# Expert blocks: rows turned a step ahead, overflow blocks with weight buffers of their own and conditional row transfers

## The reference

```python
def expert_block(args):
    xblk, e = args
    h = jax.nn.silu(xblk @ w_gate[e]) * (xblk @ w_up[e])
    return h @ w_down[e]

yb = lax.map(expert_block, (xb, blk_expert))
y = yb.reshape(P, D) * buf_gate[:, None]
return jax.ops.segment_sum(y, buf_tok, num_segments=T + 1)[:T]
```

## Time and profile before

| | |
|---|---|
| median of 3 runs | 3824.81 us (3824.13 to 3830.76) |
| the profiled execution | 3824.16 us |
| its span | 3822.2 us |
| TensorE busy (products) | 3326.4 us, 87% |
| VectorE, ScalarE, GpSimd busy | 39%, 19%, 20% |
| share of the 16 DMA engines, queue of SP | 26.9% |
| share of the 16 DMA engines, queue of POOL | 5.9% |
| expert stage of layer 0 | about 827 to 1250 us |
| expert stage of layer 1 | about 2127 to 2554 us |

### The profile page before, as it was taken

The page is one execution under the profiler, slowest core; times in us unless marked ns, Lnnn a source line. Parts: engine busy times, 40 slices in busy tenths (PEclk is TensorE's granted clock), DMA queues, the critical chain, the costliest instruction groups (busy, mean ns, idle before and its releaser), DMA issues. The chain is left out here.

```text
span 3822.2 us, 37209 instructions
## 1 busy us (share of the span) xinstructions
PE 3326.4 (87%) x14316; PEld 2289.4 (60%) x14316; DVE 1501.4 (39%) x2645; ACT 713.8 (19%) x1630; POOL 778.9 (20%) x483
## 2 busy tenths in 40 slices
PE   6979999959997499999998799936979989789996
PEld 5848666744444376676666344424757757578842
DVE  4374613320102444566654100025477631465502
ACT  1162301110011113323321000012312111111100
POOL 3213213200000330301002100012154321244300
PEclk9999999969997798899998899958989979889998
DMA  3132212228885121032222689751200121112220
GB/s 138 67 149 88 88 66 88 110 107 328 324 324 206 67 86 45 23 132 74 114 116 88 228 327 330 281 209 74 80 23 23 68 88 66 66 58 84 106 84 22
DMA packets 52388, 482.22 MB, mean 126 GB/s; under 512 B 5936, under 2 KB 6320, under 8 KB 28400
## 3 DMA queue, kind: packets, MB, share of 16 engines
q1 hardware_dynamic: 26784, 378.77, 26.9%
q0 software_dynamic: 23840, 87.04, 5.9%
q10 hardware_dynamic: 1584, 13.93, 0.9%
HBM read 507.76 MB, written 60.03 MB: 149 GB/s over the span
## 5 line engine op out<-in xcount | busy, mean ns | idle before, releaser
L573 PE MATMUL bank<-B,ring 128*128 128x256 f32 x4336 | 957.7, 382 | 37.7 <-PEq L1908 21.3
L573 PEld LDWEIGHTS bank<-B,ring 128*128 128x128 f32 x4336 | 830.8, 192 | 162.7 <-issue 49.2
L1754 PE MATMUL bank<-ring,B 128*128 128x512 f32 x1024 | 451.7, 600 | 11.5 <-issue 11.2
L557 POOL TENSOR_TENSOR ring<-ring 128x1024 f32<-128x1024 f32 x52 | 134.9, 2595 | 1255.7 <-DMA ring<-in_w_static 341.0
L573 PE MATMUL bank<-XT,ring 128*128 128x256 f32 x1344 | 308.6, 384 | 44.7 <-PEq L785 28.6
L701 ACT ACTIVATE B<-bank 128x256 f32<-128x256 f32 x356 | 135.7, 383 | 1118.9 <-PE bank L573 1095.1
L1754 PEld LDWEIGHTS bank<-ring,B 128*128 128x128 f32 x1024 | 194.1, 192 | 250.5 <-issue 232.7
L573 PEld LDWEIGHTS bank<-XT,ring 128*128 128x128 f32 x1344 | 259.3, 193 | 85.9 <-issue 51.1
L482 PE MATMUL bank<-B,ring 128*128 128x512 f32 x704 | 307.7, 596 | 2.0 <-issue 2.0
L1806 DVE TENSOR_TENSOR B<-B,bank 128x512 f32<-128x512 f32 x46 | 31.6, 688 | 579.7 <-PE bank L1754 527.6
L482 PEld LDWEIGHTS bank<-B,ring 128*128 128x128 f32 x704 | 134.9, 192 | 164.2 <-issue 163.4
(11 more groups left out here) (437 smaller groups left out, 3966.0 us busy)
## 6 DMA issues: line engine op xcount, KB each, us to landing
ring<-in_w_expert SPq DMA_DIRECT2D x138, 2048.0 KB
ring<-in_w_static SPq DMA_DIRECT2D x79, 2048.0 KB
B<-slots_x POOLq DMA_DIRECT2D x46, 512.0 KB, 9.5
slots_y<-B POOLq DMA_DIRECT2D x46, 512.0 KB, 8.8
slots_x<-B POOLq DMA_DIRECT2D x23, 512.0 KB, 15.9
ring<-s_tables SPq DMA_DIRECT2D x4, 2048.0 KB
s_tables<-tmp POOLq DMA_DIRECT2D x8, 512.0 KB, 3.8
s_tables<-B POOLq DMA_DIRECT2D x8, 512.0 KB, 3.1
```

The lines of the kernel that those rows point to most:

```text
L557: pool.tensor_tensor(s(0), w(1, 0), w(1, 1), ALU.add).then_inc(made.up(), 1)
L573: ins = pe.matmul(out, left, right, start=start and k == 0, stop=k == 3, skip_group_check=not start)
L1754: ins = pe.matmul(bank[:, :], xbT[n % 2][:, k, :], slot[:, k, :], start=k == 0, stop=k == KT - 1)
```

## The change

1. `experts`: TensorE turns the rows of block q + 1 between up of block q and down of block q - 1, and the rows of block 0 ahead of the loop. ScalarE's copies move accordingly. All instructions of a used step stay the same in number and size.
2. Weight stream: overflow chunks no longer take their turn in the ring. Gate, up and down of overflow blocks have one buffer each, three 2 MB buffers of SBUF (`B[0]`, `B[4]`, `B[5]`) that the stage doesn't otherwise use. Their order in the stream is as before, and the order of the blocks too.
3. POOL: loads of rows and stores of results of overflow blocks are issued under a condition on `block_used`, which POOL reads ahead of each (`block_in_use`). The load of block q + 2 is issued once the rows of block q are turned, and the store of block q - 2 follows it.
4. The first attention stage zeroes the overflow part of `slots_y` as well, 7 more transfers.
5. `m.routed.add(l)` stands behind the routing stage, so overflow chunks can be issued from the expert stage on only.

```diff
 def place_stream(names):
     slot, earlier, filled, kept = [], [], [], {}
-    last, total, turn = [None] * RING, [0] * RING, 0
+    last, total, turn = [None] * (RING + 3), [0] * (RING + 3), 0
     for i, n in enumerate(names):
+        if is_overflow(n):
+            at = RING + EXPERT_PART[n[0]]
+            slot.append(at)
+            earlier.append(last[at])
+            total[at] += 16
+            filled.append(total[at])
+            last[at] = i
+            continue
...
         self.ring = [sb(f"ring{i}", [P, 4096]) for i in range(RING)]
+        self.ring += [self.B[i][:, :, :].rearrange("p a b -> p (a b)") for i in (0, 4, 5)]
...
                 for n in range(N_BLOCKS):
                     pool.dma_start(m.dram["slots_x"][n * P:(n + 1) * P, :], m.B[5][:, 0:2, :]).then_inc(m.pool_dma, 16)
+                    m.pool_n += 16
+                for n in range(E_N, N_BLOCKS):
+                    pool.dma_start(m.dram["slots_y"][n * P:(n + 1) * P, :], m.B[5][:, 0:2, :]).then_inc(m.pool_dma, 16)
                     m.pool_n += 16
...
+            turn_rows(0)
+            for q in range(nb + 1):
+                if q >= 1:
+                    turn_hidden(q - 1)
+                if q < nb:
+                    gate_and_up(q)
+                if q + 1 < nb:
+                    turn_rows(q + 1)
+                if q >= 1:
+                    down(q - 1)
...
+            keep_rows(0)
+            for q in range(nb + 1):
+                if q >= 1:
+                    o = q - 1
                     act.wait_ge(*bk.made(("hT", l, o)))
                     bank = bk.bank(("hT", l, o))
                     act.activation(hidT[o % 2], bank[:, :].rearrange("p (a b) -> p a b", a=4), ACT.Copy).then_inc(bk.free_sem(("hT", l, o)), 1)
...
+                if q + 1 < nb:
+                    keep_rows(q + 1)
...
+            def load_rows(q):
+                if order[q] < E_N:
+                    pool.dma_start(xb[q % 2], rows_of("slots_x", q)).then_inc(x_in.of(q), 16)
+                else:
+                    pool.dma_start(xb[q % 2], rows_of("slots_x", q), cond=block_in_use(pool, m, order[q]),
+                                   bounds_check="skip_entire_dma").then_inc(x_in.of(q), 16)
+
+            load_rows(0)
+            load_rows(1)
+            for q in range(nb + 1):
+                if q + 2 < nb:
+                    pool.wait_ge(*bk.made(("xbT", l, q, 1)))
+                    load_rows(q + 2)
+                if q >= 2:
+                    o = q - 2
                     for i in range(2):
                         pool.wait_ge(*bk.read_done(("y", l, o, i)))
-                    pool.dma_start(m.dram["slots_y"][o * P:(o + 1) * P, :], y[o % 2]).then_inc(y_out.of(o), 16)
+                    store_rows(o)
+            for o in (nb - 1,):
+                for i in range(2):
+                    pool.wait_ge(*bk.read_done(("y", l, o, i)))
+                store_rows(o)
...
+def block_in_use(eng, m, n):
+
+    return eng.value_load(m.block_used[0:1, n - E_N:n - E_N + 1], min_val=0, max_val=1)
```

More of the change, by code:

```diff
@@ L166, in layer_chunks, with block_order, is_overflow @@
     return with_sums(names)
+def block_order():
+    return list(range(N_BLOCKS))
+BLOCK_ORDER = block_order()
 def expert_chunks(l):
     names = []
-    for n in range(N_BLOCKS):
+    for q, n in enumerate(BLOCK_ORDER):
         names += [("gate", l, n), ("up", l, n)]
-        if n:
-            names.append(("down", l, n - 1))
-    return names + [("down", l, N_BLOCKS - 1)]
+        if q:
+            names.append(("down", l, BLOCK_ORDER[q - 1]))
+    return names + [("down", l, BLOCK_ORDER[-1])]
+def is_overflow(name):
+    return name[0] in ("gate", "up", "down") and name[2] >= E_N
 S5_STREAM = [("s5_work", 0, 0), ("s5_mats", 0, 0)] + [("s5_tables", 0, _c) for _c in range(4)]
@@ L1676, in _ @@
             pool.wait_ge(m.pool_dma, m.pool_n)
-        m.routed.add(l)
         m.issue_weights(block)
+    m.routed.add(l)
 def experts(m, l):
@@ L1707, in experts, with turn_rows @@
                 for i in range(2):
-                    bk.plan(("y", l, n - 1, i), 5 + i)
+                    bk.plan(("y", l, q - 1, i), 5 + i)
         @block.tensor
         def _(pe):
-            used = None
-            for n in range(nb + 1):
+            used = {}
+            def turn_rows(q):
+                n = order[q]
                 if n >= E_N:
[L1715 to L1718, removed]
-                    for i in range(2):
[L1720 to L1728, removed]
-                    if n >= E_N:
[L1730 to L1737, removed]
-                        for k in range(4):
[L1739 to L1744, removed]
-                    for i in range(2):
[L1746 to L1778, removed]
@@ new lines, in turn_rows @@
+                    used[n] = block_in_use(pe, m, n)
+                pe.wait_ge(*x_in.at(q))
+                for i in range(2):
+                    pe.wait_ge(*bk.vacant(("xbT", l, q, i)))
+                with if_used(pe, n, used.get(n)):
+                    for i in range(2):
+                        bank = bk.bank(("xbT", l, q, i))
+                        for k in range(4):
+                            c = (4 * i + k) * P
+                            ins = pe.transpose(bank[:, k * P:(k + 1) * P], xb[q % 2][:, c:c + P], m.c("ident"))
+                        if n < E_N:
+                            ins.then_inc(bk.full_sem(("xbT", l, q, i)), 1)
@@ new lines, in turn_rows, with turn_hidden @@
+                if n >= E_N:
+                    for i in range(2):
+                        signal(pe).then_inc(bk.full_sem(("xbT", l, q, i)), 1)
+            def turn_hidden(q):
+                n = order[q]
+                pe.wait_ge(*m.tally("hidden_values").at(q + 1))
+                pe.wait_ge(*bk.vacant(("hT", l, q)))
+                bank = bk.bank(("hT", l, q))
+                with if_used(pe, n, used.get(n)):
+                    for k in range(4):
+                        ins = pe.transpose(bank[:, k * P:(k + 1) * P], hid[q % 2][:, k * P:(k + 1) * P], m.c("ident"))
+                    if n < E_N:
+                        ins.then_inc(bk.full_sem(("hT", l, q)), 1)
+                if n >= E_N:
+                    signal(pe).then_inc(bk.full_sem(("hT", l, q)), 1)
@@ new lines, in gate_and_up @@
+            def gate_and_up(q):
+                n = order[q]
+                for i in range(2):
+                    pe.wait_ge(*bk.read_done(("xbT", l, q, i)))
+                for what, kind in (("g", "gate"), ("u", "up")):
+                    pe.wait_ge(*m.landed((kind, l, n)))
+                    slot = m.slot_of((kind, l, n))[:, :].rearrange("p (k f) -> p k f", k=8)
+                    pe.wait_ge(*bk.vacant((what, l, q)))
+                    bank = bk.bank((what, l, q))
+                    with if_used(pe, n, used.get(n)):
+                        for k in range(KT):
+                            ins = pe.matmul(bank[:, :], xbT[q % 2][:, k, :], slot[:, k, :], start=k == 0, stop=k == KT - 1)
+                        if n < E_N:
+                            ins.then_inc(bk.full_sem((what, l, q)), 1)
+                    if n >= E_N:
+                        signal(pe).then_inc(bk.full_sem((what, l, q)), 1)
+                    m.last_use((kind, l, n), (what, l, q))
@@ L2951, in _ @@
             act.wait_ge(m.pool_dma, m.pool_n)
-            for i in range(RING):
+            for i in range(RING + 3):
                 act.wait_ge(m.ring_full[i], max(f for f, at in zip(m.filled, m.slot_at) if at == i))
```

93 lines of the change are left out of this document (54 added, 39 removed).

## The result

| | before | after |
|---|---|---|
| median, 4 runs each | 3824.47 us | 3769.04 us (3765.84 to 3774.10) |
| the profiled execution | 3824.16 us | 3767.88 us |
| its span | 3822.2 us | 3766.2 us |

The ratio is 0.9853 (95% interval 0.9836 to 0.9870): faster by 55.4 us. The forecast was 3787 with a range to 3773.

The account below looks back on a forecast made before the run. TensorE was taken to bound the loop over used blocks, transfers close behind; 11.2 us from the used steps, 14.7 from layer 0's tail and 11.5 from layer 1's sum to 37.4 off 3824.16, giving 3787 us, range 3773 to 3803.

Parts of the forecast that it names:

- The used steps: Expert loop: turning rows ahead removes 0.40 us of TensorE's wait a step, 11.2 us over 14 steps of 2 layers.
- The overflow steps: Expert tail: SP's flag reads and issues set 5.25 us a step, three chunks at 1.75 each.
- Rival (D): Expert tail: a chunk costs SP 2.15 us, not 1.75, making each tail 6.4 longer; 3800 us, chance 0.10.
- The end of the store: Expert tail, layer 0: the skipped last store lands in 1.0 us, not 10.7, and POOL goes on at 1231.1.
- Rival (B): End of the expert stage: the skipped store still reports behind the next layer's prefetch; 3798 us, chance 0.15.
- The drain: End of the expert stage: first gather 4.9 us behind the last store's landing, 3.8 of these POOL's drain.
- The gathers against the early chunks: Gathers after the experts: prefetched chunks' remaining transfer takes back 3.5 us in layer 0, 9.9 in layer 1.
- rival (E): Gathers after the experts: they don't feel the prefetch, so 13.4 us more are gained; 3774 us, chance 0.05.
- Rival (C): Expert loop: no gain, the gap moves to another wait or transfers hold the step at 22.5; 3798 us, chance 0.12.
- (F): Expert tail: conditional transfers make POOL drain before each flag read, 6.3 us each; slower, 3842 us, chance 0.05.
- Zeroing costs nothing: First attention stage: seven more zeroing transfers cost nothing, as POOL idles until 282.67; without that cover 11 us once.
- The conditions named for being wrong: Conditional transfer holds POOL over 2 us, first gather still follows the prefetch's end, or used step stays at 22.5.

Follow-up runs that it names:

- e3: The changed kernel with only the rows turned ahead: overflow chunks back in the ring, row transfers unconditional, no extra zeroing; 3793.24 us, ratio 0.9915 to before.
- e4: The changed kernel with rows turned in their own step as before, the rest of the change kept; 3793.72 us, ratio 0.9916 to before.
- e6: The changed kernel with the next layer's chunks held back until the second stage of the combination; 3762.75 us, ratio 0.9829 to before.
- e7: The kernel before with the next layer's chunks held back until the second stage of the combination; 3811.50 us, ratio 0.9950 to before.

## Why the prediction was too small

The places and the waits were right; what failed are the sizes of terms in the sum. The largest is the transfer of the early chunks against the gathers, booked with no overlap at 3.5 + 9.9 = 13.4 us where 0.4 + 5.9 = 6.3 came, then the gap in the used steps, 0.40 a step where 0.59 came. All points have the same sign; in brackets are the us by which the gain of layer 0 / layer 1 was larger than the sum had it.

**The used steps (3.3 / 2.6).** The mechanism was right, the size was not: 0.40 a step was taken, 0.59 came. The choice of "a little above the lower row", for one more change between transposes and products, had no row behind it. The step of after holds the same changes and is busy for its full 21.91 us; the wait on the weight load (0.56) was the price. That is 0.19 by 14, or 2.7; the rest lies ahead of block 15, where the layers of before differ by 1.9 too.

**The overflow steps (1.0 / 0.9).** Right: SP is late next, TensorE's ring of 4.1 opens. The sum had 16 chunks by 1.75, 0.6 of waiting and 0.6 of signals, 29.2 us from the gate signals of block 17. By SP's and TensorE's timelines it was 27.0 and 1.3, 28.3. A chunk costs 1.55 and a step 4.65. Of the 2.2 that this leaves 1.3 is SP's wait for TensorE before the last chunk, and 0.9 is in two chunks that took longer, one of them by a slow flag read of 0.84 us among 16 (SP's reads of block_used, ns min, median, max):

```profile
L412 SPq TENSOR_LOAD <-block_used x16: 262/266/842, 1197.1 to 1222.6; - x16
```

The 1.75 of the earlier trace rows was from six chunks in a row of before: by SP's timeline three of the five steps between them are 1.55 and two 2.0 to 2.1, with slower flag reads in both (up to 0.78 us). So the mean was right for them and too long as a price for all. Rival (D) went the other way and fell. What the prediction missed is that turning rows ahead would by itself have hidden the row transfers: the gain was counted once and is reached by two ways (e3, e4).

**The end of the store (1.3 / 1.6).** POOL is past its wait at 1227.4, 2.6 us behind the last signals, where 3.9 was booked. The issue comes 1.95 behind the last signals where 2.8 was booked: VectorE's copies start 0.3 before these signals end, and from the copies' end flag read and issue take 1.0 us and not 1.5. The landing takes at most 0.65 and not 1.0. Rival (B) fell on this: with two chunks of 2 MB issued at 1223.55, a report behind them would have come with their landing, at 1231.4 to 1236.6, and POOL's wait ended at 1227.4. In e6 and after the wait is equally short, with and without chunks under way. The rule of the Trainium skill, DMA: Bandwidth & Descriptors, section "Why a DMA increments its semaphore by 16 and not by 1", has all 16 engines post for a transfer issued from GpSimd; a skipped one is reported here without queueing behind what these engines are moving, so the measurement speaks against reading that rule as a wait.

**The drain (1.1 / 1.1).** The sum kept 4.9 us from landing to gather. It is 3.7, as the drain takes 2.67 instead of 3.80. It follows the form of POOL's last transfers: 2.84 to 2.86 to the stage's end in all kernels with conditional rows, 3.96 or 3.97 in all without, held chunks or not.

**The gathers against the early chunks (3.1 / 4.0).** That the chunks delay the gathers is shown (e6, e7), but it was priced at the full time that the chunks still need, 3.5 and 9.9; measured 0.4 and 5.9. The chunks' landing in after, layer 0 and layer 1 (min, median, max in us from issue):

```profile
DMA to landing us min/median/max: 7.9/10.2/12.6
...
DMA to landing us min/median/max: 8.0/12.6/18.2
```

The last chunk lands at 1236.6, 5.5 behind the first gather's issue, and in layer 1, issued at 2491.9, at 2510.1, 11.9 behind it. The stage of the gathers grew by 0.4 and 5.9, less than a tenth of the 5.5 and half of the 11.9. The stretches show why (the gathers of before, those of after in layer 0, then layer 1 with chunks under way and behind them; columns as above), with SP's queue q1 and POOL's q0 from 2501 to 2509 (packets, MB, share):

```profile
1257.00:1263.00 6.00, 0.00 (x0) 0.00 (x0) 0.00 (x0) 0.00 (x0) 4.52 (x5) 0.50 0.96 311
...
1236.00:1244.00 8.00, 0.00 (x0) 0.00 (x0) 0.00 (x0) 0.00 (x0) 3.75 (x4) 0.50 1.02 412
...
2501.00:2509.00 8.00, 0.00 (x0) 0.00 (x0) 0.00 (x0) 0.00 (x0) 5.41 (x6) 0.50 0.99 419
2509.00:2517.00 8.00, 0.00 (x0) 0.00 (x0) 0.00 (x0) 0.00 (x0) 0.00 (x0) 0.50 1.02 415
...
q1 hardware_dynamic: 191, 2.74, 79.9%
q0 software_dynamic: 165, 0.61, 18.7%
```

In before the eight gathers move 4.2 MB in 15.1 us, 277 GB/s; at the 415 GB/s of the later rows 10.1 us would do. (Why they are slower alone the rows don't say: the DMA share is 0.96 at 311 GB/s in the first.) In after chunks and gathers together keep the engines at 412 to 419. At the first gather's issue 1.65 MB of chunks were left in layer 0 and 3.98 in layer 1 (the rest of SP's queue in the trace), 4.0 and 9.6 us at 415 GB/s, and in both layers 3.6 to 3.7 us of that vanish, since the gathers behind them move faster than they do alone. So the steps of the forecast that failed are to let nothing overlap, and to take the rate of a stretch bound by TensorE, 326 GB/s, for what the transfers can do. While chunks last, a gather gets little (0.61 of 3.35 MB above), but it is not shut out. For layer 0 rival (E) was right within 0.4; for layer 1 the truth lies between it and the forecast.

**The rest.** 1.7 us in layer 1 is from laying the two tails over each other by one instruction: down of block 15 lay 1.5 earlier in layer 1 by that clock. Together the points give some 22 us; the clock pattern of the first attention stage took 5.7 back and other stages gave 2.5, which leaves 18.6. Rival (C) fell (21.91), and so did (F): a conditional transfer takes POOL 0.93 us (1225.86 to 1226.79), from the flag read to the end of the issue of 0.04, with no drain, where 1.54 was taken. "Zeroing costs nothing" was not contradicted.

The range was too narrow for one reason: nearly every choice was taken on the cautious side, and the lower end took in (E) alone (13.4) or the loop's upper bound alone (4.5), not both. Both together make 3769, the measured time, but by luck: (E) held for one layer only, and the rest of the gain came from terms that had no bounds. The conditions named for being wrong were all about mechanisms, and none of them came.

## What to carry to other kernels

Where transfers are skipped by a flag, what is left of their price is the issuing queue's reading of flags: read each flag once, and ask who issues before adding buffers (three of 2 MB brought nothing here, where no overflow block was used; whether they pay when one is, no run shows). A prefetch sent at the end of a stage stands ahead of that stage's last store and the next one's gathers; its cost is found by holding it back in one run. It is less than its own time where the transfers behind it are slow by themselves (0.4 of 4.0 us, 5.9 of 9.6). And where a stall has a row with a price, book the whole row unless another row says what stays.

## What the runs showed that was not expected

- A skipped conditional transfer of POOL costs 0.04 us of issue (0.93 with its flag read), and its wait is over within 0.65 us, with 4 MB under way on the other queue.
- POOL's drain at the end of the stage is 2.67 us behind conditional transfers and 3.80 behind plain ones. No run says why, nor whether it is the condition or that nothing was moved.
- The granted clock of the attention stages changes between executions of like kernels (1.00 or 0.74 to 0.78 in one stretch), and with it their length, from 88 to 97 us.
- Eight gathers of 512 KB by themselves move 277 GB/s from the first issue to the last landing (4.2 MB in 15.1 us); behind other transfers the DMA engines go on at 412 to 415.
